# Moving two of twelve modulation tiles from the first stage to the second, and one zeroing from VectorE to GpSimd

## The reference, cut to what matters

```python
def second_block(x, c, w_ada, b_ada, ...):
    mod = jax.nn.silu(c) @ w_ada[l] + b_ada[l]        # 1024 x 6144 matrix, one row
    sh1, sc1, g1, sh2, sc2, g2 = jnp.split(mod[:, None, :], 6, axis=-1)
    hn = (_rms(x, norm1_g[l]) * (1 + sc1) + sh1).astype(x.dtype)
    y = _mixer(hn, w_in[l], ...)
    x = x + g1 * (y @ w_out[l])
    ...
```

## Time and profile before

| what | value |
|---|---|
| device time, median of 3 runs | 2456.46 us (2454.93 to 2461.7) |
| device time of the profiled execution | 2454.93 us |
| its span, first to last instruction | 2453.2 us |
| mean granted TensorE clock | 0.917 of full speed |
| busy: PE, DVE, POOL, ACT | 84%, 70%, 43%, 25% of the span |
| mean DMA rate | 276 GB/s |

### The profile page before, as it was taken

The page is one execution under the profiler, slowest core; times in us unless marked ns, Lnnn a source line. Parts: engine busy times, 40 slices in busy tenths (PEclk is TensorE's granted clock), DMA queues, the critical chain, the costliest instruction groups (busy, mean ns, idle before and its releaser), DMA issues. The chain is left out here.

```text
span 2453.2 us, 25460 instructions
## 1 busy us (share of the span) xinstructions
PE 2068.3 (84%) x7721; PEld 1309.7 (53%) x7721; DVE 1705.4 (70%) x3529; ACT 611.1 (25%) x1443; POOL 1043.3 (43%) x1085
## 2 busy tenths in 40 slices
PE   6987888897768787777889877777797898999999
PEld 6955565454333343434544433333336875788887
DVE  7947488777877866777677878787757574544464
ACT  2134234432222211113112232322211332110121
POOL 0000066665676776677666666667660000000000
PEclk9996989999888998989999989888998998999999
DMA  7841199999999999999999999999994302233222
GB/s 262 310 137 69 29 321 362 335 352 356 354 368 407 363 378 402 395 393 386 361 404 402 405 392 357 360 359 363 373 367 150 136 18 69 80 91 103 68 90 98
DMA packets 260633, 676.44 MB, mean 276 GB/s; under 512 B 19501, under 2 KB 107938, under 8 KB 260514
## 3 DMA queue, kind: packets, MB, share of 16 engines
q0 software_dynamic: 147456, 536.94, 57.7%
q1 hardware_dynamic: 113058, 138.07, 16.8%
HBM read 672.81 MB, written 2.10 MB: 275 GB/s over the span
## 5 line engine op out<-in xcount | busy, mean ns | idle before, releaser
L2569 PE MATMUL bank<-arena 128*128 128x512 f32 x1568 | 829.2, 664 | 186.1 <-DMA arena<-in_peer_v,arena 90.3
L2790 DVE SCALAR_TENSOR_TENSOR arena<-arena,h_ps 128x1024 f32<-128x1024 f32 x512 | 612.0, 1216 | 145.8 <-DMA arena<-in_peer_u,arena 97.3
L2526 POOL DMA_INDIRECT arena<-in_peer_v,arena x512 | 515.0, 1006 | 322.3 <-issue 138.3
L2526 POOL DMA_INDIRECT arena<-in_peer_u,arena x512 | 512.0, 1000 | 237.0 <-issue 151.5
L2569 PEld LDWEIGHTS bank<-arena 128*128 128x128 f32 x1568 | 308.8, 210 | 549.4 <-issue 394.4
L2804 DVE SCALAR_TENSOR_TENSOR x<-arena,x 128x1024 f32<-128x1024 f32 x120 | 154.3, 1286 | 45.5 <-DMA arena<-in_peer_v,arena 29.2
L2650 ACT ACTIVATE arena<-ident,arena 128x128 f32<-128x128 f32 x392 | 138.7, 393 | 69.1 <-PE bank L2569 19.0
L1605 PE MATMUL bank<-hT,arena 128*128 128x256 f32 (+1 forms) x576 | 125.7, 374 | 10.3 <-issue 10.3
L142 DVE CAST parts<-arena 128x2048 fp32r<-128x2048 f32 (+5 forms) x61 | 67.5, 1107 | 89.2 <-DMA arena<-in_w_gate_up 75.4
L144 DVE TENSOR_TENSOR parts<-arena,parts 128x2048 fp32r<-128x2048 f32 (+5 forms) x61 | 125.4, 2056 | 4.9 <-issue 0.4
L1605 PEld LDWEIGHTS bank<-hT,arena 128*128 128x128 f32 x576 | 106.3, 204 | 38.5 <-issue 27.1
(11 more groups left out here) (476 smaller groups left out, 3243.4 us busy)
## 6 DMA issues: line engine op xcount, KB each, us to landing
arena<-in_w_ada SPq DMA_DIRECT2D x12, 2048.0 KB, 10.7
arena<-in_w_in SPq DMA_DIRECT2D x15, 1536.0 KB, 7.4
arena<-in_w_gate_up SPq DMA_DIRECT2D x44, 512.0 KB, 5.0
arena<-in_peer_w_q SPq DMA_DIRECT2D x16, 1024.0 KB, 7.9
arena<-in_w_down SPq DMA_DIRECT2D x22, 512.0 KB, 3.5
arena<-in_peer_u,arena POOLq DMA_INDIRECT x512
arena<-in_peer_v,arena POOLq DMA_INDIRECT x512
arena<-in_w_in SPq DMA_DIRECT2D x7, 1024.0 KB
```

Source lines behind the costliest of these rows:

```text
L2526: nc.gpsimd.indirect_dma_start(out=row, out_offset=None, in_=a[table][0], in_offset=bass.IndirectOffsetOnAxis(ap=expert[:, s % TB, j:j + 1 ...
L2569: ins = nc.tensor.matmul(psum[half][:, :], diag[:, m % R, :], row[:, half * 512:(half + 1) * 512], start=(s % PH == 0 and j == 0), stop=(s ...
L2790: nc.vector.scalar_tensor_tensor(out=u_ring[:, n % R, :], in0=u_ring[:, n % R, :], scalar=1.0, in1=h_ps[:, :], op0=ALU.mult, op1=ALU.mult, ...
```

## The change

Two things are changed.

`ADA_EARLY` falls from 10 to 8. Column tiles 3 and 4 of the first stage carry one modulation tile each instead of two, and the second stage has four tiles, t = 8 to 11, where it had two. Tiles 8 and 9 are loaded there without a wait (`t % ADA_EARLY >= 2` is false for them); tiles 10 and 11 wait for the sums of tiles 8 and 9.

The zeroing of `gate_of[0].bias` moves from DVE to POOL, right ahead of the iota, with the wait for `q_copied` and a second one for `sc_summed`. DVE keeps its own wait for `sc_summed` and the zeroing of `w_g_a`. The thresholds of `gates_zeroed` fall by one.

```diff
-        ADA_EARLY = 10
+        ADA_EARLY = 8
...
-        ADA_AT = {1: (0, 1), 2: (2, 3), 3: (4, 5), 4: (6, 7), 5: (8, 9)}
+        ADA_AT = {1: (0, 1), 2: (2, 3), 3: (4,), 4: (5,), 5: (6, 7)}
...
         def place_w_g(act, t):
...
-            act.wait_ge(gates_zeroed, 2)
+            act.wait_ge(gates_zeroed, 1)
...
-                    act.wait_ge(gates_zeroed, 3)
+                    act.wait_ge(gates_zeroed, 2)
...
             if slot == I0 + 6:
-                dve.wait_ge(q_copied, 2 * PH + 2)
                 dve.wait_ge(sc_summed, 2 * PH + 2)
-                nc.vector.memset(gate_of[0].bias, 0.0).then_inc(gates_zeroed, 1)
                 nc.vector.memset(w_g_a, 0.0).then_inc(gates_zeroed, 1)
...
                         if i == 2 * PH + 5 and j == 0:
-                            pool.wait_ge(gates_zeroed, 1)
+                            pool.wait_ge(q_copied, 2 * PH + 2)
+                            pool.wait_ge(sc_summed, 2 * PH + 2)
+                            nc.gpsimd.memset(gate_of[0].bias, 0.0)
+                            pool.drain()
                             nc.gpsimd.iota(gate_of[0].bias[0:SM_H, :], [[1, GT]], base=0, channel_multiplier=0,
```

## The result

The changed kernel takes 2473.17 us (median of 5 runs, 2469.62 to 2479.81), the kernel before 2456.46 us (five runs by then, with the same median and range). The ratio is 1.0068, 95% interval [1.0051, 1.0086], which is +16.7 us. The forecast was 2463 us with a range up to 2470: a slowdown was what I held for nearly as likely as no change, and its size was missed.

The account below looks back on a forecast made before the run. PE was taken to bound the first two stages, with a serial chain behind to the gathers. −1.70 + 6.55 + 1.7 + 0.1 = +6.65 us on the median of 2456.46 gave 2463 us, range 2455 to 2470.

Parts of the forecast that it names:

- First part: First stage: two fewer PE turns, behind column tiles 3 and 4, save 0.85 us each, −1.70 us.
- Second part: Second stage: four tiles instead of two use up DVE's slack of 7.2 us and start the attention later, +6.55 us.
- the last turn's cold 0.85: End of second stage: PE's last turn, behind a pause, runs at 1.2 GHz and costs up to 0.85 us more.
- The clock: After PE's new pause: last turn and first transposes run at 1.2 GHz, +1.7 us, bounds 0 and +2.1.
- Third part: Zeroing on POOL ahead of the iota: memset and drain mostly covered by outstanding gathers, +0.1 us, bounds −0.3 and +1.57.
- The claim that all is in series: From second stage through attention to the gathers: a microsecond lost before 173 us arrives at the gathers and the end.
- A: Second stage: the two late loads are slow, 11.5 and 14.5 us; +12.85 us in all, 2469.3 us; chance 0.15.
- B: Attention: the full clock returns in a later stretch and pays back 8 us, giving −1.35, 2455 us; chance 0.12.
- C: Behind 180 us: a late transfer or wait absorbs the 8 us delay, leaving −1.70, 2454.8 us; chance 0.05.

Follow-up runs that it names:

- experiment 2: Kernel before with eight early modulation tiles instead of ten, zeroing left on DVE: 2378.41 us, ratio 1.0036.
- experiment 8: Changed kernel with its drain replaced by a semaphore that the memset counts up, against the kernel before: 2454.86 us, ratio 1.0032.
- experiment 5: Changed kernel again without edit, on the second chip, beside the kernel before: 2456.02 us, ratio 1.0046.
- experiment 11: Kernel before run once more without edit, one execution for a profile: 2439.69 us.
- experiment 9: Kernel before with one drain on POOL ahead of step 1 of the gathers: 2443.04 us, ratio 1.0018.
- experiment 1: Kernel before with only the zeroing moved to POOL, followed by the drain, early tiles as before: 2373.74 us, ratio 1.0016.
- experiment 3: Kernel before with one drain added on POOL between its wait and the iota, memset left on DVE: 2376.82 us, ratio 1.0027.
- experiment 4: Kernel before with the zeroing on POOL, ordered before the iota by a semaphore instead of a drain: 2365.73 us, ratio 0.999.
- experiment 6: Kernel before with drains on POOL ahead of the gathers of steps 14, 21 and 27, zeroing on DVE: 2471.21 us, ratio 1.0097.
- experiment 7: Kernel before with a drain on POOL ahead of the very first gather: 2447.99 us, ratio 1.0001.
- experiment 10: Kernel before with nine early tiles, three in the second stage, and zeroing on POOL ordered by semaphore, no drain: 2445.57 us, ratio 1.0011.

## Why the prediction was wrong, step by step

**First part, −1.70 us: right.** The second stage starts earlier: the up projections' row of L1039 is at 136.39 us in the changed kernel, 139.08 in the kernel before. That is 2.7 us; 1.7 of it is the two turns, and the rest lies within what the start of the program differs by between executions (137.87 to 139.50 in the eight traces with ten early tiles). On average the four traces with eight early tiles have that row 1.3 us earlier than those eight.

**Second part, +6.55 us: right in mechanism, too small by 1 to 2 us.** Forecast, from the kernel before's start: a wait of 2.1 us for the third load (2.03), none for the fourth (none), landings of 8.3 and 8.0 us (8.1 and 8.0), about 5 us of waiting on PE (4.38; 5.19 and 4.95 in experiments 2 and 8), L1221 near 177.8 us (178.49; 180.80 and 179.50). From the first row of L1039 to L1221 it is 42.1 to 42.3 us in the four traces with eight early tiles and 32.5 to 33.9 in the eight with ten: 8.8 us more on average, where 7.4 were forecast with the last turn's cold 0.85. Most of what was missed is the stage's first tile: it landed in 12.3 us instead of the 11.5 of the earlier trace rows, and DVE starts on it 13.3 to 13.7 us behind L1039, where it was 12.0 to 13.1 with ten.

**The clock, +1.7 us: right in kind.** In the first trace it fell one turn earlier than I had said, with the pause of 1.56 us ahead of the turn of tile 10; that turn lies beside DVE's last sum and costs nothing. The last turn ran at 1.2 GHz in all four executions and cost 1.0 us more. From L1221 to the first gather it is 1.3 us more on average with eight early tiles (129.6 to 132.4 us against 128.9 to 130.7). The mean granted clock of that stretch was 0.73 in the changed kernel's first trace and 0.78 in that of the kernel before, but 0.76 and 0.79 in experiments 5 and 2, so a slower attention as a whole is not shown. The Trainium skill (TensorE: Matmul & The Clock Gate, section HAM oscillation) warns of matmul bursts between waits for DMA, which start cold; here PE waited for DVE, and the trace agrees, with 1.87 us for a turn that takes 0.85 us at the full clock. The first two parts and the clock together were forecast at +6.55 us, and measured at +8.8 on average at the first gather, and at the end at +7.9 and +9.3.

**Third part, +0.1 us with an upper bound of 1.57: this step failed.** It cost about 10 us where it stands: 64 gathers take 108.7, 106.9, 105.3 and 109.0 us in the four kernels with the one drain, 97.2 to 99.7 in the eight traces without a drain at this place. The forecast said that gathers outstanding would cover POOL's standstill. It is the reverse: they are what the drain waits for. I priced the drain from the last line of the earlier trace rows, where the idle time around it is 0.15 us; nothing of POOL's own was on its way there. It was a row of the same instruction in the other state.

And the price that I missed stood in the first line of the same group. POOL's idle time of 11.09 us ahead of the memset at 1848.49 is put down to POOL's own queue at L2477, the edge between two stages. In the trace of the next run of this kernel (experiment 11) a drain's record with that line ends just ahead of the memset: 1831.53 against 1831.77, with 9.29 us of idle time. In the kernel before POOL's last gather is this one (timeline of POOL):

```profile
1836.08 1.31 POOL L2526 DMA_INDIRECT arena<-in_peer_v,arena  x1 [0.30 <-issue]
```

It is issued by 1837.39. The last gather bytes move at 1843.31, 5.9 us later, and the drain's record ends at 1848.25, 4.9 us behind them. The DMA share is high until 1847 (0.87 from 1846), but that is other traffic: from 1843.4 to 1848.2 the only queue that moved anything was

```profile
q1 hardware_dynamic: 1294, 1.30, 84.5%
```

So the gathers account for the first 5.9 of the 11.09 us, and the rest is the same unexplained tail as in the table of experiment 9, only longer. It does not go by the number of gathers since the drain before it either, 1024 here. The row would still have given the third part 11 us of standstill in place of 0.4. I had read this idle time as one of another kind and taken the group for its last number. Nor is it quite free where it stands: DVE, the last of the other engines, was done at 1847.33, so the kernel before loses about 0.9 us to it (1.0 in experiment 11).

The working of the 10 us. Between the last bytes of the old gathers and the first of the new ones lie 4.0 us (1323.0 to 1327.0), and the tail before it and the start behind it, at partial share, are worth some 3 us more: by the share of 1.03, the 20 us from 1307 to 1327 with 0.75 lack 5.4 us and those from 1327 to 1347 with 0.95 lack 1.6. The refilling is slow, since POOL issues a gather each 1.24 us (1326.15, 1327.41, 1328.65 and so on) while the DMA engines need 1.30 us for one (0.524 MB at 402 GB/s). The other 3 us I could not put on one cause; PE and DVE stood for 3 us with nothing, and PE then worked at a clock of 0.56.

**How much of it reaches the end.** By the medians it is +3.2 and +6.3 us against the kernel before (experiments 1 and 3), 8.0 in the pair of drain and semaphore (1 and 4), 8.6 for each of three (6) and 1.2 in the pair 5 and 8; each has an uncertainty of several microseconds. The traces add a sharper measure, the time from the 641st gather to the last:

| | without the drain | with it |
|---|---|---|
| first measurement | 568.6 | 579.7 |
| experiments 1 to 4 | 532.4, 532.9 | 540.7, 543.1 |
| experiments 5 and 7 to 11 | 562.6 to 565.1 | 573.1 |

That is 8 to 11 us, so nearly all of the local 10 us is still there at the last gather. For the three drains of experiment 6 it is 1054.5 us from the 321st gather to the last, against 1026.3 to 1033.1 in experiments 7 to 11. Behind the gathers little is given back: from the last one to the end it is 614.7 to 616.6 us in the four traces with the one drain and 615.3 to 622.3 in those without. Tiles at 8 to 9 us and a drain at 8 to 11 make 16 to 20, which is the +16.7 of the changed kernel. The +10.5 of experiment 5 is below that, with an interval that reaches 17.9; why its median is lower is open.

**The claim that all is in series: right in the main.** The delay of the second stage reached the first gather and the end in every kernel with eight early tiles, as far as the spread of the times can tell.

**The rivals.** A (slow late loads) did not happen: 8.1 and 8.0 us. B (the clock pays back) did not: in the first trace the full clock came back 63 us behind L1221 where it had been 61, later and not earlier. C (absorbed) did not: the tiles alone cost 7.9 us. The right rival, a drain as a wait for POOL's own DMAs, was not among them, although `pool.drain()` stood in the diff.

## What to carry to other kernels

In every run here a drain on POOL did not end before all the gathers that POOL had issued had moved their last byte. To order a memset ahead of the next instruction on that engine, count a semaphore up on it and wait for that count. Where an instruction is priced from a row elsewhere, ask what was outstanding on its engine there: an idle queue and a full one are two prices. In a trace, a long idle time that ends in "issue" means that a sequencer instruction without a row may stand there; look it up in the program. And an experiment that adds an instruction to see its price must put it where nothing else hides it.

## What the runs showed of the hardware

- A drain on POOL ended only after the last bytes of the gathers issued before it: 0.04 us with none, 5.55 us of idle time with 0.71 MB still to move, 9.5 with 1.16 and 13.5 to 16.3 with 2 to 3.9. It ended 1.0 to 2.3 us after the last gather byte in seven of eight cases and 4.4 us in the other (experiment 6), and 4.9 and 4.7 us at the stage's edge in the kernel before (its first trace and experiment 11). What it waits for in that time, and whether a drain on another engine behaves so, wasn't tried.
- The drain's record starts at 1306.18 us, 2.6 us before the memset ahead of it runs. The Trainium skill (Perfetto Trace Analysis, section Per-engine timelines) says that the record of a sequencer-only instruction starts when all its semaphores are satisfied. The drain waits for none, and the trace agrees as far as it goes: the record starts ahead of a gather and the memset, which stand before the drain in the program. So its length, 19.13 us, is not what it costs.
- The kernel before took 2370.55 us on one chip, 2445.56 and 2441.74 on another, and 2456.46 in the first measurement. Nearly all of that lies in the gathers: from the first to the last it took 1445.5 us in experiment 4, on the first of these chips, and 1518.9 in experiment 11, on the second. Over some 400 us of that stage experiment 4 moved 402 GB/s on the first of these chips and experiment 11 moved 374 on the second. Ratios are to be taken on one chip.
